# Two attentions in a transformer kernel: padded low keys, one normalisation for eight heads, another order on the tensor engine

## The reference

```
_gqa_scores(q, k) = einsum("bqhgd,bkhd->bhgqk", q, k) * HEAD_DIM ** -0.5      # 8 query heads, 2 key heads of 64
_sink_softmax(scores, sink):
    m = max(max(scores), sink);  e = exp(scores - m)
    return e / (sum(e) + exp(sink - m))
_windowed_attention: queries in blocks of 128; keys: the neighbouring blocks within |i - j| <= 128, and 256 context keys
_global_attention:   queries in blocks of 128; keys: all 512 tokens and the 256 context keys; plain softmax
```

## Time and profile before

| | us |
|---|---|
| median of 3 runs | 1998.08 (1994.54 to 1999.4) |
| profiled execution, span | 2000.1 |
| PE busy in it | 1881.0 (94%) |
| DVE, ACT, POOL busy | 1146.5, 640.3, 753.5 |
| second attention, first product to the end of the last values | 1246.57 to 1462.3 |

### The profile page before, as it was taken

How to read it: one execution, slowest core, us unless ns; L and a number is a source line. 1 busy time by engine, 2 the same in 40 slices (tenths; PEclk the granted TensorE clock), 3 DMA queues, 4 the chain that set the end, 5 groups by cost and what they waited for, 6 DMA issues and landing times. The chain is left out here.

```text
span 2000.1 us, 25465 instructions
## 1 busy us (share of the span) xinstructions
PE 1881.0 (94%) x8737; PEld 1522.2 (76%) x8737; DVE 1146.5 (57%) x1807; ACT 640.3 (32%) x1053; POOL 753.5 (38%) x368
## 2 busy tenths in 40 slices
PE   6889999989979999999999998999999699999995
PEld 5778878877756788888887887777777487887874
DVE  6882874866994344244243294445568865354467
ACT  3111211232455332122223235454421343232222
POOL 3344443447660244444444443000024134444443
PEclk8899999999889899999999999999999799999997
DMA  7453562544211133333323332000012123233311
GB/s 229 145 162 111 168 180 83 170 125 114 60 48 33 43 95 95 113 94 103 95 74 111 100 92 77 1 1 1 1 42 85 42 84 114 87 103 90 98 57 42
DMA packets 279112, 178.31 MB, mean 89 GB/s; under 512 B 6200, under 2 KB 258292, under 8 KB 278900
## 3 DMA queue, kind: packets, MB, share of 16 engines
q1 hardware_dynamic: 264320, 149.20, 25.6%
q10 hardware_dynamic: 14708, 28.03, 4.3%
HBM read 175.11 MB, written 2.10 MB: 89 GB/s over the span
## 5 line engine op out<-in xcount | busy, mean ns | idle before, releaser
L593 POOL TENSOR_TENSOR wL<-raw,wH 128x1024 fp32r<-128x1024 f32 (+2 forms) x280 | 683.4, 2445 | 1201.0 <-ACT wH L1087 1200.2
L655 PE MATMUL ps<-actH,wH 128*128 128x512 f32 x1280 | 508.0, 397 | 15.8 <-DVE actL L1804 5.6
L655 PE MATMUL ps<-actL,wH 128*128 128x512 f32 x1280 | 503.9, 394 | 0.0
L655 PE MATMUL ps<-actH,wL 128*128 128x512 f32 x1280 | 503.7, 393 | 0.0
L1087 ACT ACTIVATE wH<-raw 128x1024 fp32r<-128x1024 f32 (+2 forms) x280 | 286.1, 1030 | 462.6 <-PE ps L655 453.4
L655 PEld LDWEIGHTS ps<-actH,wH 128*128 128x128 f32 x1280 | 243.8, 190 | 73.2 <-issue 9.6
L655 PEld LDWEIGHTS ps<-actH,wL 128*128 128x128 f32 x1280 | 243.8, 190 | 51.6
L655 PEld LDWEIGHTS ps<-actL,wH 128*128 128x128 f32 x1280 | 244.3, 191 | 49.6
L655 PE MATMUL ps<-hidH,wH 128*128 128x512 f32 x656 | 261.1, 398 | 20.0 <-DVE hidL L1430 7.2
L655 PE MATMUL ps<-hidH,wL 128*128 128x512 f32 x656 | 259.4, 395 | 0.0
L655 PE MATMUL ps<-hidL,wH 128*128 128x512 f32 x656 | 258.7, 394 | 0.0
(11 more groups left out here) (289 smaller groups left out, 2307.4 us busy)
## 6 DMA issues: line engine op xcount, KB each, us to landing
mod_raw<-in_w_mod ACTq DMA_DIRECT2D x24, 1024.0 KB, 5.2
raw<-in_w_in SPq DMA_DIRECT2D x48, 512.0 KB, 3.7
raw<-in_ffn_w_gate SPq DMA_DIRECT2D x44, 512.0 KB, 3.8
raw<-in_ffn_w_up SPq DMA_DIRECT2D x44, 512.0 KB, 3.8
raw<-in_w_up SPq DMA_DIRECT2D x44, 512.0 KB, 3.8
raw<-in_ffn_w_down SPq DMA_DIRECT2D x32, 512.0 KB, 3.8
raw<-in_w_out SPq DMA_DIRECT2D x16, 512.0 KB, 3.9
raw<-in_w_down SPq DMA_DIRECT2D x16, 512.0 KB, 3.8
```

What stands on the lines that cost most here:

```text
L593: nc.gpsimd.tensor_tensor(wL[:, a:a + w], raw[:, a:a + w], wH[:, a:a + w].bitcast(F32), ALU.subtract).then_inc(lo_ready, 1)
L655: return nc.tensor.matmul(out, a, b, start=first, stop=last)
```

## The change

- The low keys get a buffer for each branch, `kLA` and `kLB`. The half that has no low keys is set to zero by POOL, ahead of the first lows of the stage `merge`; PE waits for it before the second attention. The low product now reads all 128 partitions of `q` and of the low keys. `kLB` lies over the rotary tables `ropeT` and `biasx`.
- PE's order for unit n becomes `logits(n + 2)`, `turn(n)`, `values(n - 1)`, in both attentions.
- The transposed blocks are split by half between ACT (bank 4) and DVE (bank 5): of 1, 2, 3, 4, 5, 6 blocks ACT copies 1, 1, 1, 2, 2, 3.
- The values of eight heads go side by side into one bank (6 or 7, by query block). One reciprocal of 8 columns and one multiply of 512 columns scale them all, after the second unit of the next block.
- The sinks of eight heads take one addition on DVE and one exponential on ACT, where each head had its own exponential and addition.

```diff
@@ -247,14 +247,16 @@
     gain2 = sb("gain2", 2 * DH)
-    ropeT = sb("ropeT", 4 * ST * DH)
+    region("rope", 4 * ST * DH + 512)
+    ropeT = at("ropeT", ("rope", 0), 4 * ST * DH)
+    biasx = at("biasx", ("rope", 4 * ST * DH), 512)
     sink = sb("sink", 2 * NH)
-    biasx = sb("biasx", 512)
...
-    kL = at("kL", ("free", 8320 - NKV * (CTX + S)), NKV * (CTX + S), F32R)
+    kLA = at("kLA", ("free", 8320 - NKV * (CTX + S)), NKV * (CTX + S), F32R)
+    kLB = at("kLB", ("rope", 0), NKV * (CTX + S), F32R)
...
@@ -393,12 +397,9 @@
...
                            v=[v1[:, b * ATT + head * DH:][:, 0:DH] for b in range(tile + 1)],
-                           out=attn1[:, tile * ATT + head * DH:][:, 0:DH], sink=None)
-
+                           out=attn1[:, tile * ATT:(tile + 1) * ATT], sink=False)
...
@@ -418,15 +419,15 @@
                     products.append((at_col, [(q[:, a:a + P], kH[:, key:key + w]),
-                                              (q[high, a:a + P], kL[high, key:key + w])]))
+                                              (q[:, a:a + P], kL[:, key:key + w])]))
                     at_col += w
                 yield dict(W=P * len(blocks), products=products, col0=col0, mask=mask,
                            v=[v[:, b * NKV * DH + kv * DH:][:, 0:DH] for b in blocks],
-                           out=out[:, tile * ATT + head * DH:][:, 0:DH], sink=head if banded else None)
+                           out=out[:, tile * ATT:(tile + 1) * ATT], sink=banded)
 
     group1 = list(units1())
-    group2 = list(units2(qA, kHA, lower, vA, attnA, True)) + list(units2(qB, kHB, upper, vB, attnB, False))
+    group2 = list(units2(qA, kHA, kLA, vA, attnA, True)) + list(units2(qB, kHB, kLB, vB, attnB, False))
@@ -454,8 +455,10 @@
-    wide = [u["W"] > 512 for u in group1 + group2]
-    WIDE = [sum(wide[:n]) for n in range(len(wide) + 1)]
+    blocks_of = [u["W"] // P for u in group1 + group2]
+    BY_ACT = [max(1, nb // 2) for nb in blocks_of]
+    V_TURNS = [sum(nb > 1 for nb in blocks_of[:n]) for n in range(len(blocks_of) + 1)]
+    GROUPS1, GROUPS2 = len(group1) // NH, len(group2) // NH
@@ -630,6 +633,12 @@
             else:
+                if st["name"] == "merge":
+                    pool.wait_ge(q2_rot, 1)
+                    pool.wait_ge(lo_ready, st["base"])
+                    for low, half in ((kLA, upper), (kLB, lower)):
+                        G.memset(low[half, :].bitcast(F32), 0.0).then_inc(low_zero, 1)
+                    pool.wait_ge(low_zero, 2)
@@ -899,22 +908,23 @@
                 pe.wait_ge(probs, n + 1)
                 if n > 0:
                     pe.wait_ge(probT_a, n)
-                if n > n0 and units[n - 1 - n0]["W"] > 512:
-                    pe.wait_ge(probT_v, WIDE[n])
+                if V_TURNS[n] > 0:
+                    pe.wait_ge(probT_v, V_TURNS[n])
                 for b in range(u["W"] // P):
-                    mm = nc.tensor.transpose(bank(4 + b // 4, P, (b % 4) * P),
-                                             prob[:, (n % 3) * 768 + b * P:][:, 0:P], ident)
+                    into = bank(4, P, b * P) if b < BY_ACT[n] else bank(5, P, (b - BY_ACT[n]) * P)
+                    mm = nc.tensor.transpose(into, prob[:, (n % 3) * 768 + b * P:][:, 0:P], ident)
                 mm.then_inc(prob_T, 1)
 
             def values(n):
                 u = units[n - n0]
+                g, head = n // NH, n % NH
                 pe.wait_ge(probT_a, n + 1)
-                if u["W"] > 512:
-                    pe.wait_ge(probT_v, WIDE[n + 1])
-                if n >= 2:
-                    pe.wait_ge(attn_out, n - 1)
+                if V_TURNS[n + 1] > 0:
+                    pe.wait_ge(probT_v, V_TURNS[n + 1])
+                if head == 0 and g >= 2:
+                    pe.wait_ge(attn_out, g - 1)
                 for b, v in enumerate(u["v"]):
-                    mm = product(bank(6 + n % 2, DH), probT[:, (n % 2) * 768 + b * P:][:, 0:P], v,
+                    mm = product(bank(6 + g % 2, DH, head * DH), probT[:, (n % 2) * 768 + b * P:][:, 0:P], v,
                                  b == 0, b == len(u["v"]) - 1)
                 mm.then_inc(pv, 1)
@@ -923,9 +933,9 @@
             logits(n0 + 1)
             warm(5)
             for n in range(n0, end):
-                turn(n)
                 if n + 2 < end:
                     logits(n + 2)
+                turn(n)
...
         pe.wait_ge(q2_lo, len(TURNS2))
+        pe.wait_ge(low_zero, 2)
@@ -1216,20 +1227,21 @@
                 u = units[n - n0]
                 act.wait_ge(logit, n + 1)
                 c = n % 32
-                if u["sink"] is not None:
-                    link(nc.scalar.activation(stat[:, 64 + c:65 + c], stat[:, c:c + 1], ACT.Exp,
-                                              bias=sink[:, u["sink"]:u["sink"] + 1]))
                 p = prob[:, (n % 3) * 768:][:, 0:u["W"]]
                 nc.scalar.activation(p, p, ACT.Exp, scale=-1.0, bias=stat[:, c:c + 1],
                                      accum_out=stat[:, 32 + c:33 + c]).then_inc(probs, 1)
 
             def copy(n):
-                u = units[n - n0]
-                w = min(512, u["W"])
+                w = BY_ACT[n] * P
                 act.wait_ge(prob_T, n + 1)
                 if n >= 2:
                     act.wait_ge(pv, n - 1)
                 nc.scalar.activation(probT[:, (n % 2) * 768:][:, 0:w], bank(4, w), ACT.Copy).then_inc(probT_a, 1)
+
+            def sink_terms(g):
+                a = 64 + (g * NH) % 32
+                act.wait_ge(sink_sum, g - n0 // NH + 1)
+                nc.scalar.activation(stat[:, a:a + NH], stat[:, a:a + NH], ACT.Exp).then_inc(sink_exp, 1)
 
             end = n0 + len(units)
             exps(n0)
@@ -1237,6 +1249,8 @@
                 if n + 1 < end:
                     exps(n + 1)
                 copy(n)
+                if n % NH == NH - 1 and units[n - n0]["sink"]:
+                    sink_terms(n // NH)
 
         attention(group1, 0, prob1, probT1)
@@ -1615,43 +1629,50 @@
                     dve.wait_ge(prob_T, n - 2)
                 b = 2 * (n % 2)
                 src = ps[:, b:b + 2, :].rearrange("p b n -> p (b n)")[:, u["col0"]:u["col0"] + u["W"]]
-                start = 3e38 if u["sink"] is None else sink[:, NH + u["sink"]:][:, 0:1]
+                start = sink[:, NH + n % NH:][:, 0:1] if u["sink"] else 3e38
                 V.tensor_tensor_reduce(out=prob[:, (n % 3) * 768:][:, 0:u["W"]], in0=src, in1=u["mask"],
                                        scale=-(DH ** -0.5), scalar=start, op0=ALU.add, op1=ALU.min,
                                        accum_out=stat[:, c:c + 1]).then_inc(logit, 1)
 
-            def sums(n):
-                u, c = units[n - n0], n % 32
-                dve.wait_ge(probs, n + 1)
-                total = stat[:, 32 + c:33 + c]
-                if u["sink"] is not None:
-                    link(V.tensor_tensor(total, total, stat[:, 64 + c:65 + c], ALU.add))
-                link(V.reciprocal(stat[:, 96 + c:97 + c], total))
+            def sink_terms(g):
+                a = (g * NH) % 32
+                dve.wait_ge(logit, (g + 1) * NH)
+                V.tensor_tensor(stat[:, 64 + a:64 + a + NH], stat[:, a:a + NH], sink[:, 0:NH], ALU.add).then_inc(sink_sum, 1)
 
             def copy(n):
-                u = units[n - n0]
-                if u["W"] > 512:
+                u, first = units[n - n0], BY_ACT[n] * P
+                if u["W"] > first:
                     dve.wait_ge(prob_T, n + 1)
-                    dve.wait_ge(pv, n - 1)
-                    V.tensor_copy(probT[:, (n % 2) * 768 + 512:][:, 0:u["W"] - 512],
-                                  bank(5, u["W"] - 512)).then_inc(probT_v, 1)
-
-            def out(n):
-                u, c = units[n - n0], n % 32
-                dve.wait_ge(pv, n + 1)
-                V.tensor_scalar(u["out"], bank(6 + n % 2, DH), stat[:, 96 + c:97 + c], None, ALU.mult).then_inc(attn_out, 1)
+                    if n >= 2:
+                        dve.wait_ge(pv, n - 1)
+                    V.tensor_copy(probT[:, (n % 2) * 768 + first:][:, 0:u["W"] - first],
+                                  bank(5, u["W"] - first)).then_inc(probT_v, 1)
+
+            def normalise(g):
+                u, a = units[g * NH - n0], (g * NH) % 32
+                dve.wait_ge(probs, (g + 1) * NH)
+                total, inverse = stat[:, 32 + a:32 + a + NH], stat[:, 96 + a:96 + a + NH]
+                if u["sink"]:
+                    dve.wait_ge(sink_exp, g - n0 // NH + 1)
+                    link(V.tensor_tensor(total, total, stat[:, 64 + a:64 + a + NH], ALU.add))
+                link(V.reciprocal(inverse, total))
+                dve.wait_ge(pv, (g + 1) * NH)
+                V.tensor_tensor(u["out"].rearrange("p (h d) -> p h d", h=NH),
+                                bank(6 + g % 2).rearrange("p (h d) -> p h d", h=NH),
```

(23 more changed lines are left out.)

## The result

Over four runs the changed kernel has a median of 1943.68 us (1943.45 to 1945.07) beside 1998.74 (1994.54 to 2002.02) for the kernel before in the same comparison: ratio 0.9733, interval 0.9716 to 0.9751. In a later comparison with more runs the ratio was 0.9738. The forecast was 1944.

A forecast was written before the change was run, and what follows sets the result against it. PE's own stream was taken to bound both attentions. Savings of 41.7 + 13.0 + 1.2 - 0.8 = 55.1 us took the median 1998.08 to 1943, plus one for DVE stalls: 1944, range 1937 to 1958 (8 in 10).

The forecast's parts named there:

- The product term: Second attention, padded low keys: 216 256-wide products save 41.7 us, 64 512-wide save 13.0, reaching the dense rate.
- The order: Logits ahead of transposes, both attentions: adds no PE instruction, so 0, within 1 us either way.
- The start: First eight products of the second attention, at the low clock: 1.2 us saved, between 0 and 2.2.
- The ends: Last multiply of each attention becomes 512 wide, near 0.69 instead of 0.28, on the path twice: -0.8 us.
- Copies, grouped scaling: Halved copies and scaling of eight heads at once: covered by PE's period, lateness below 2 us in all.
- Zeroing: Two POOL memsets ahead of merge's lows, between 0.5 and 2.5 us each: nothing on PE's path.
- First attention: Its logits stay 64-row, so it lasts the same as before within 1 us.
- The load hides: Rival, padded products: the weight load no longer hides, only 25 us saved, so 1973; chance 0.04.
- DVE is not the bound: Rival: DVE bounds the short 512- and 640-wide banded units, 21.6 us not gained, so 1965; chance 0.09.
- The clock stayed at 1.00: Rival: second attention at the low clock; slower from a share of 0.46, 2062 us for the whole; chance 0.02.

The follow-up runs named there:

- transposes first: Changed kernel with PE's order of before (transposes, then logits two units ahead, then values) in both attentions: 1941.65 us, ratio 0.9720; repeated 1940.55 us, 0.9722.
- grouped products: Kernel before, 64-row products kept, each global unit's two high-key logit products run before its two low-key ones instead of alternating: 1983.12 us, ratio 0.9934.

## Why the prediction was right

*The product term.* Predicted 41.7 + 13.0 = 54.7 us; measured about 51.4. That is the second attention's 55.5, plus 0.5 for the later end, less 4.6 at the start, which is priced below. The products themselves have the predicted prices, 0.12 and 0.23, but for the first of each unit, which takes 0.32 (0.20 in branch A, where it has 256 columns). With the transposes first the unit is 2.64 against 2.63 predicted, since the transposes then give back what this product takes. So the term was right, and what is missing belongs to the order.

*The order.* Predicted 0, within 1 us either way. It costs 0.055 in each of 64 units, 3.5 us before what the start and the ends give back; 3.1 measured (160.2 against 157.1). The bound of 1 us was wrong. The reason given, that only waits could change, left out that the step from one kind of product to the next has a price of its own.

*The start.* Predicted 1.2, at most 2.2; measured 4.6, the part of the prediction that was farthest off. The eight products went from 4.08 to 1.87 us as computed (0.23 each against 0.24). The ten passes behind them were to give part of this back, on the assumption that the clock rises 10 us after PE began, as in the earlier trace rows. It rose about 3 us after, and the passes took 4.51 instead of 7.31 (1250.65 to 1257.96 in the trace of before). Up to the end of the passes 5.0 are gained (6.4 us instead of 11.4). Behind them some 0.3 go again in the first logit product, which takes 0.52 instead of 0.20, and some 0.3 in a wait ahead of the second transposes. So the start gave between 4.4 and 5.0; 4.6 is taken. The bound of 2.2 supposed that the passes could not become faster, and no row supported that. Nor is all of it the padding's doing: in the kernel with grouped products this start is instruction for instruction that of before, and there too the clock rose earlier. The windows of its eight products and its ten passes:

```profile
1242.79:1246.87 4.08, 4.08 (x9) 2.29 (x9) 0.76 (x2) 1.01 (x3) 0.00 (x0) 0.50 0.00 0
1246.87:1252.51 5.64, 5.64 (x12) 2.45 (x12) 0.76 (x2) 1.20 (x5) 0.00 (x0) 0.78 0.00 0
```

The passes took 5.64 there instead of 7.31, so 1.7 us of the start can come without any edit to it.

*The ends.* Predicted 0.8 for both together; 0.47 each, so 0.9. Right.

*Copies, grouped scaling.* Predicted to be covered, with up to 2 us of stalls. PE's idle time in the steady part is 0.11 us. That the cover is real but thin shows in the kernel with padding alone, which has the old copies and waits in every second 512-key unit.

*Zeroing.* Predicted 0.5 to 2.5 each and nothing on the path. It took 1.38 each, and PE has no wait for it.

*First attention.* Predicted unchanged within 1 us; it is 1.7 shorter. The kernel with padding alone, whose code there is that of before, takes 62.3, so 2.2 of before's 64.5 is a clock that fell at 652 there and later elsewhere. Beside that kernel the changed one is 0.5 longer, which is its later end. Its new order gains some 0.6 up to the last seven units, but the clock, which fell at 651.5 instead of 654.8, takes as much back in those seven (6.3 us instead of 5.7).

*The rivals.* The load hides: a load costs 0.107 (12 in 1.28), and at 0.12 a product of 256 columns there is no room for it. The Trainium skill's rule of overlap only between different row groups (TensorE: Matmul & The Clock Gate, section "Part 3: Packing small matmuls") does not hold here, where all rows are the same. DVE is not the bound. The clock stayed at 1.00 in the steady part.

In sum the mechanism and the main term were right: the steps between row counts went, at the price read from the rows. That the time came out within 1 us is luck, since two misses of 3 us met: the order cost what the start gave. Outside the second attention, too, differences of -0.6, -1.7, +1.5 and -0.4 us add up to no more than -1.3; the two larger ones are mostly the clock.

## What to carry to other kernels

Where a chain of matmuls alternates between 64 and 128 rows, look at the starts of consecutive ones: if each is 0.2 us behind the dense rate, fill the short operand with zeros or group the products by row count. Do the cheapest part of such a change by itself and time it: here the padding alone gave the whole gain, and with the rest of the change the two attentions took 2.3 us more. When two kernels differ by a few us, look at the granted clock of stretches that they share before explaining it.

## What the runs showed of the hardware that was not expected

- A change between 64-row and 128-row products costs 0.20 us at the 2.4 GHz level, for rounded halves and plain fp32 alike: 3.43 to 3.03 for two changes fewer, 1.99 to 1.60 for two others. At the 1.2 GHz level it is 0.30 (the first products of the second attention, with one change each, follow at 0.51 before and 0.21 after).
- After the same idle time of 4.3 us, PE was at the high level again 10 us after its first product in the kernel before and about 3 us after it in the changed one. All ten traces of kernels with padded low keys have some 3.4 us of low clock around this start; the three without them (before, all but the padding, products grouped) have 10, 10 and 7. So padding goes with the earlier rise, but the grouped kernel's 7 came with a start that is the same as before's; what decides it was not tried apart.
- After one and the same wait of 2.6 us the clock fell in some kernels and stayed in others, and in these places the repeated traces of a kernel agree (two each of the changed kernel, padding alone and transposes first). Each such stretch is worth about 1.5 us, together up to 6 us of a run here.
